# Index products with the roles of their operands exchanged, places computed in the layout of their own item, and the product for the rows to fetch moved between two blocks of matmuls

## What is computed

```python
h = rmsnorm(x, norm1); proj = h @ w_in
x = x + concat(diff_attention(q, k, v), pool_mixer(p)) @ w_out
h = rmsnorm(x, norm2)
logits = h @ w_router + b_router            # 32 experts
topv, topi = top_k(logits, 4); gates = softmax(topv)
for each expert e, for its tokens:          # exact, none dropped
    g = min(h @ w_gate[e] + b_gate[e], 7);  u = clip(h @ w_up[e] + b_up[e], -7, 7)
    y = ((u + 1) * g * sigmoid(1.702 * g)) @ w_down[e] + b_down[e]
    x[token] += gate * y
out = rmsnorm(x, final_norm)
```

## Time and profile before

| | us |
|---|---|
| median of three runs | 2234.3 (2232.83 to 2234.88) |
| span of the profiled execution | 2233.1 |
| TensorE matmuls busy | 2168.6 (97%) |
| VectorE busy | 645.9 |
| ScalarE busy | 613.1 |
| GpSimd busy | 460.4 |

### The profile page before, as it was taken

One profiled execution on the slowest core, in us unless ns is written; L12 is line 12 of the kernel. 1 busy time (PEld: TensorE's weight loads), 2 busy tenths in 40 slices (PEclk: granted clock), 3 DMA queues, 4 the chain that ended last, 5 costly groups with the idle time before them and its releaser, 6 DMA issues.

```text
span 2233.1 us, 30784 instructions
## 1 busy us (share of the span) xinstructions
PE 2168.6 (97%) x10323; PEld 1007.6 (45%) x10324; DVE 645.9 (29%) x1868; ACT 613.1 (27%) x1208; POOL 460.4 (21%) x491
## 2 busy tenths in 40 slices
PE   8999999996999999999999899999999999999996
PEld 4444577543444344344434434434443444444443
DVE  2100599255322223121122212212112221222223
ACT  2000588311222322222223222322123221322223
POOL 1014011223121212212121221221122112122222
PEclk9999999997999999999999999999999999999998
DMA  7100300335568967858869795793889968677775
GB/s 265 44 36 0 116 1 1 103 122 207 201 202 296 361 223 245 303 172 325 304 214 363 229 371 190 246 363 112 328 314 373 359 225 283 252 254 263 258 263 187
DMA packets 150889, 501.08 MB, mean 224 GB/s; under 512 B 10570, under 2 KB 35935, under 8 KB 150303
## 3 DMA queue, kind: packets, MB, share of 16 engines
q1 hardware_dynamic: 115184, 445.20, 51.9%
q0 software_dynamic: 33792, 50.35, 11.0%
q10 hardware_dynamic: 1874, 5.02, 0.6%
HBM read 461.64 MB, written 43.09 MB: 226 GB/s over the span
## 4 chain that ended last, share of the span: by engine, by line
PE 93%; DMA 3%; DVE 2%; issue 1%; ACT 1%; POOL 0%; DVEq 0%; ACTq 0%; SPq 0%; POOLq 0%
PE psum L1566 41%; PE psum L1604 15%; PE psum L1294 10%; PE psum L1355 5%; PE psum L1615 4%; PE psum L1378 3%; PE psum L1344 3%; PE psum L1473 2%; DMA weights<-in_w_down 2%; PE psum L1574 2%; PE psum L1554 1%; PE psum L1627 1%; PE psum L1639 1%; PE psum L1387 1%; DMA weights<-in_w_up 1%
## 5 line engine op out<-in xcount | busy, mean ns | idle before, releaser
L1566 PE MATMUL psum<-weights,work 128*128 128x512 f32 (+2 forms) x3008 | 950.4, 595 | 0.0
L1566 PEld LDWEIGHTS psum<-weights,work 128*128 128x128 f32 (+2 forms) x3008 | 365.8, 159 | 487.6 <-issue 487.2
L642 POOL DMA_INDIRECT residual_rows<-work x184 | 287.6, 1563 | 457.2 <-ACT work L856 410.7
L1604 PE MATMUL psum<-weights,work 128*128 128x512 f32 x768 | 340.0, 595 | 0.0
L598 POOL DMA_INDIRECT work<-normed_rows,work x48 | 49.4, 1030 | 839.9 <-DVE work L1095 778.9
L1294 PE MATMUL psum<-weights 128*128 128x512 f32 x512 | 220.9, 593 | 1.3 <-DVE weights L928 1.3
L1604 PEld LDWEIGHTS psum<-weights,work 128*128 128x128 f32 x768 | 142.1, 190 | 166.2 <-issue 166.2
L1184 DVE TENSOR_SCALAR work<-psum 128x256 f32<-128x256 f32 x188 | 79.7, 424 | 417.8 <-ACT work L825 415.0
L825 ACT ACTIVATE work<-psum 128x256 f32<-128x256 f32 x188 | 71.9, 383 | 379.6 <-PE psum L1566 359.6
L807 ACT ACTIVATE work<-psum 128x512 f32<-128x512 f32 x96 | 57.6, 600 | 426.6 <-PE psum L1473 426.6
L1294 PEld LDWEIGHTS psum<-weights 128*128 128x128 f32 x512 | 96.8, 190 | 122.0 <-issue 120.4
(11 more groups left out here) (214 smaller groups left out, 1708.5 us busy)
## 6 DMA issues: line engine op xcount, KB each, us to landing
weights<-in_w_gate SPq DMA_DIRECT2D x64, 2048.0 KB
weights<-in_w_up SPq DMA_DIRECT2D x64, 2048.0 KB
weights<-in_w_down SPq DMA_DIRECT2D x64, 2048.0 KB, 10.4
weights<-in_w_in SPq DMA_DIRECT2D x8, 768.0 KB, 14.2
residual_rows<-x SPq DMA_DIRECT2D x9, 512.0 KB, 3.8
normed_rows<-work ACTq DMA_DIRECT2D x9, 512.0 KB, 3.9
x<-in_x SPq DMA_DIRECT2D x8, 512.0 KB, 9.6
bias_rows_repeated<-bias_rows SPq DMA_DIRECT2D x4, 1024.0 KB, 10.1
```

The lines of the kernel that those rows point to most:

```text
L642: pl.indirect_dma_start(acc_d[:, :], bass.IndirectOffsetOnAxis(dest[:, b:b + 1], 0), yrow[:, b * BLK:(b + 1) * BLK], None, compute_op=ALU. ...
L1566: mm = pe.matmul(out.rearrange("p (m n) -> p m n", m=2), xT[:, k, lo:lo + cols], wgu[:, :, k, blk * BLK:(blk + 1) * BLK], start=False, sto ...
L1604: mm = pe.matmul(bank(4 + h), actT[:, k, :], wdn[:, k, h * HALF:(h + 1) * HALF], start=False, stop=(k == DT - 1))
```

## The change

- `index` exchanges the operands: the six columns are stationary, `pickT` moves (128 columns). The eight products are laid side by side in the 128*32 mode, four at a time, in two rounds, and leave four partial sums in partitions 32g to 32g+5, by 128 slots. The six columns of the expert come from a fixed buffer `parts_own`, which VectorE fills before each `compare` (one copy more).
- `spread_index` is gone. The 128x128 results are copied to `parts_next`, and one item later to `parts_now`. `own_places` multiplies slices of `parts_now` (stationary) with a few columns of ones and zeros `sel`, only for the layout of the item in hand, between `rows(0)` and `index`: 1 product for 128 tokens, 2 for 64, 2 and 4 for 96, 4 for 32.
- A new product `next_rows` (stationary `parts_next`, 128 columns, one moving column) sums the parts of the token number. It stands between `gate_up_ends(0)` and `gate_up_ends(1)`. `row_numbers` follows it on VectorE, ahead of the four units instead of behind them.
- Before item 0, the row numbers of item 1 have eight products of their own, and places of item 0 are computed inside item 0.
- After the loop, the last item computes its places in VectorE's straight part.

```diff
+            def index(n, own=parts_own, picks=pickT, at=6):
+                pe.wait_ge(s_pick, n + 1)
+                if not isinstance(n, int) or n > 0:
+                    pe.wait_ge(s_own, n)
+                for r in range(2):
+                    for g in range(4):
+                        i = 4 * r + g
+                        mm = pe.matmul(index_out(at)[32 * g:32 * g + 6, :],
+                                       own[:, i, :], picks[:, i, :], start=(r == 0), stop=(r == 1))
+                mm.then_inc(s_ips, 1)
...
+                def place_of(blocks, slots, cols):
+                    n = slots.stop - slots.start
+                    for g in range(P // n):
+                        mm = pe.matmul(places_out[n * g:n * g + n, blocks, :].rearrange("p b c -> p (b c)"),
+                                       parts_now[:, slots], sel[:, cols], start=True, stop=True)
+                    return mm
+
+                def own_places():
+                    if tokens == 128:
+                        mm = place_of(slice(0, 4), slice(0, 128), slice(0, 8))
+                    if tokens == 96:
+                        place_of(slice(0, 2), slice(0, 64), slice(0, 4))
+                        mm = place_of(slice(2, 4), slice(64, 96), slice(6, 10))
+                    if tokens == 64:
+                        mm = place_of(slice(0, 4), slice(0, 64), slice(4, 12))
+                    if tokens == 32:
+                        mm = place_of(slice(0, 4), slice(0, 32), slice(6, 14))
+
+                def next_rows():
+                    pe.wait_ge(s_idxb, j + 3)
+                    pe.wait_ge(s_xT, 2 * j + 3)
+                    pe.matmul(next_out, parts_next, sel[:, 0:1], start=True, stop=True).then_inc(s_gps2, 1)
...
-                pe.wait_ge(s_found, j + 1)
-                spread_index(j + 1)
...
                 rows(0)
-                pe.wait_ge(s_found, j + 2)
-                index(j + 2, bass.ds(e2, 1)).then_inc(s_ips, 1)
+                pe.wait_ge(s_idxb, j + 2)
+                pe.wait_ge(s_found, 2 * j + 2)
+                own_places()
+                index(j + 2)
...
                     gate_up_ends(0)
+                    next_rows()
                     gate_up_ends(1)
```

On VectorE, in the loop:

```diff
-                    places(chain, j + 1, kind)
-
+                    dve.wait_ge(s_ips, j + 3)
+                    places(chain, kind)
+                    chain(dve.tensor_copy(parts_now, parts_next))
+                    dve.tensor_copy(parts_next, index_out(6)).then_inc(s_idxb, 1)
+
+                    dve.wait_ge(s_gps2, j + 1)
+                    row_numbers(chain, next_out)
                     for b in range(UNIT):
-                        if b == 0:
-                            dve.wait_ge(s_ips, j + 3)
-                            index_parts(j + 2)
                         unit(j, b)
-
-                    dve.wait_ge(s_xtp, 2 * j + 3)
-                    row_numbers(chain, idxb[:, 0:3])
+                    dve.wait_ge(s_found, 2 * j + 4)
                     dve.wait_ge(s_added, j + 1)
-                    chain(dve.tensor_copy(dest, nextitem[:, 0:4]))
-                    chain(dve.tensor_copy(dgate, nextitem[:, 4:8]))
-                    shift_places(j + 1)
+                    chain(dve.tensor_copy(dest, later[:, 0:4]))
+                    dve.tensor_copy(dgate, later[:, 4:8]).then_inc(s_dest, 1)
                     item_slots(chain, bass.ds(e3, 1), bass.ds(j + 3, 1))
+                    own_parts(bass.ds(e3, 1)).then_inc(s_own, 1)
                     compare()
```

More of the change, by code:

```diff
@@ L183, in encoder_kernel @@
         idx = small(1).bitcast(U32)
[L184 to L188, removed]
+        new, empty = small(1), small(1)
+        parts_now, parts_next = (small(CHUNK // 2).bitcast(BF16) for _ in range(2))
+        found, lost, later = small(4), small(4), small(8)
         dest = small(4).bitcast(U32)
         dgate = small(4)
-        tables = small(24 + 2 * EXPERTS)
+        tables = small(40 + 2 * EXPERTS)
         place, away, of_row = tables[:, 0:12], tables[:, 12:24], tables[:, 24:24 + EXPERTS]
         of_place = tables[:, 24 + EXPERTS:24 + 2 * EXPERTS]
+        sel_rows = tables[:, 24 + 2 * EXPERTS:]
         items = small(3 * TABLE)[0:1, :].bitcast(I32)
@@ L1089, in compare, with own_parts @@
                                   col.unsqueeze(2).to_broadcast([P, TT, CHUNK]), ALU.is_equal).then_inc(s_pick, 1)
+            def own_parts(e):
+                return dve.tensor_copy(parts_own.rearrange("p i c -> p (i c)"),
+                                       parts_e[:, e, :, :].rearrange("p e i c -> p (e i c)"))
             def row_numbers(chain, src):
-                chain(dve.tensor_reduce(new, src, AX_X, ALU.add))
-                chain(dve.scalar_tensor_tensor(empty, new, 1.0, missing, ALU.is_lt, ALU.mult))
@@ L1094, in row_numbers @@
-                chain(dve.scalar_tensor_tensor(new, new, -1.0, empty, ALU.add, ALU.add))
+                chain(dve.scalar_tensor_tensor(empty, src, 1.0, missing, ALU.is_lt, ALU.mult))
+                chain(dve.scalar_tensor_tensor(new, src, -1.0, empty, ALU.add, ALU.add))
                 dve.tensor_copy(idx, new).then_inc(s_idx, 1)
[L1097 to L1110, removed]
+            def first_row_numbers(src):
+                link(dve.tensor_reduce(new, src, AX_X, ALU.add))
+                row_numbers(link, new)
@@ L1111, in places @@
+            def places(chain, kind):
+                chain(dve.scalar_tensor_tensor(lost, places_out[:, :, 0], 1.0, away[:, bass.ds(kind * 4, 4)],
                                                ALU.is_lt, ALU.mult))
-                chain(dve.scalar_tensor_tensor(found[:, 0, :], found[:, 0, :], float(UNIT),
+                chain(dve.scalar_tensor_tensor(found, places_out[:, :, 0], float(UNIT),
                                                place[:, bass.ds(kind * 4, 4)], ALU.mult, ALU.add))
-                chain(dve.tensor_tensor(later[:, 0:4], found[:, 0, :], lost, ALU.add))
@@ L1222, in _, with last_step @@
             last = dve.value_load(total[0:1, 1:2], min_val=EXPERTS - 1, max_val=MAX_ITEMS - 1)
-            dve.wait_ge(s_rps, n_items + 1)
-            dve.sem_inc(s_found, 1)
+            kind = dve.value_load(items[0:1, bass.ds(n_items + (2 * TABLE - 1), 1)], min_val=0, max_val=KINDS - 1)
+            ended = [0]
+            def last_step(ins):
+                ended[0] += 1
+                ins.then_inc(s_ldve, 1)
+                dve.wait_ge(s_ldve, ended[0])
+            dve.wait_ge(s_ips, n_items + 2)
+            places(last_step, kind)
+            dve.sem_inc(s_idxb, 1)
+            dve.sem_inc(s_idx, 1)
             unit(last, 0)
             unit(last, 1)
+            dve.wait_ge(s_found, 2 * n_items + 2)
             dve.wait_ge(s_added, n_items)
[L1228 to L1231, removed]
+            last_step(dve.tensor_copy(dest, later[:, 0:4]))
+            dve.tensor_copy(dgate, later[:, 4:8]).then_inc(s_dest, 1)
             unit(last, 2)
@@ L1474, in row_transposes @@
                 mm.then_inc(s_xtp, 1)
[L1477 to L1495 removed]
             pe.wait_ge(s_tokid, 3)
             pe.wait_ge(s_lgt, TT)
[L1499 removed]
+            first_rows(0, slice(0, 1), pick0, rows_out)
             pe.wait_ge(s_diag, 4)
```

107 lines of the change are left out of this document (48 added, 59 removed).

## The result

The changed kernel takes 2240.83 us (median of 7 runs, 2239.39 to 2241.61) against 2234.3 before: a ratio of 1.0029, 95% interval 1.002 to 1.0038. The forecast was 2239.4, range 2231 to 2247, with slower as the likeliest case. The profiled execution took 2241.5, of which 2239.3 is its span; before it was 2233.1, so the spans differ by 6.2.

The account below looks back on a forecast made before the run. TensorE, busy 97% of the span, was taken as the bound. Terms -8.3 + 7.4 + 8.5 - 1.2 - 1.3 = +5.1 us on the 2234.3 median gave 2239.4 us; own range 2234 to 2245, 8-in-10 range 2231 to 2247.

Parts of the forecast that it names:

- spread removed: Dropping eight spread products at item boundaries saves 0.18 behind 128 tokens, 0.28 behind 64 or 96, nothing behind 32: -8.3 us.
- places and index: From an item's last transpose to its long product, new place products, index and mode changes add +7.4 us, bounds +3 to +12.
- product for the rows: The added `next_rows` product costs 0.11 in full items, 0.25 between narrow blocks, 0.27 in items of 32: +8.5 us.
- start: Before and in item 0, VectorE's places no longer awaited, item 1's gather an estimated 1.7 earlier: -1.2 us, between -0.5 and -3.
- last item: In the last item the index no longer waits for VectorE's loop exit nor runs 0.76 longer than usual: -1.3 us.
- the 0.33 to 0.40 named as a sign: Expected profile sign: distance from a full item's places to the next long product is 0.33 to 0.40 us.
- The wait ahead of item 0: Expected profile sign: TensorE's wait before item 0 gone, and the one for the gather longer.
- The cheap change (1): Mode changes behind products this short are cheap, at 0.05 us the sum is +0.5: 2235 us; chance 0.14.
- The index in a fourth of the time (2): Four tiles at once make eight index products take 0.05 instead of 0.15, 4.7 us less: 2234.7; chance 0.08.
- Tiles that don't overlap (3): Eight bfloat16 index products run one after another, 0.3 more in each of 47 items, +13: 2252 us; chance 0.04.
- `next_rows` waits (4): `next_rows` holds TensorE's queue for `parts_next`, 0.6 in 8 items, unit 0 as late: +5 to +8, 2246; chance 0.11.
- More from start and end (5): Wait before item 0 gives all 3.0, the end 2, 2.5 beyond the booked; with cheap mode changes 2232 us; chance 0.05.

Follow-up runs that it names:

- again: The changed kernel run once more, unaltered; 2239.86 us, ratio 1.003 to the kernel before.
- no_spread: The kernel before without the eight spread products in its items, a wait and a semaphore increment in their place; 2229.04 us, ratio 0.9981.
- fewer_waits: The changed kernel with one implied TensorE wait at an item's start dropped and another moved behind the rows' transposes; 2238.59 us, ratio 1.002.
- places_last: The changed kernel with the place products behind the eight index products instead of ahead of them; 2238.57 us, ratio 1.0018.
- moved: The changed kernel with the rows product straight ahead of the hidden transposes, in another bank, and row numbers after unit 0; 2233.91 us, ratio 1.0001.
- order: The changed kernel with only VectorE's order altered: row numbers worked out after unit 0 instead of before it; 2242.02 us, ratio 1.0037.
- behind: The changed kernel with the rows product left in place but in another bank with its waits, row numbers after unit 0; 2241.38 us, ratio 1.0032.

## Why the prediction was right, point by point

| Step | booked | measured |
|---|---|---|
| spread removed | -8.3 | -7.2 |
| places and index | +7.4 | +5.6 |
| product for the rows | +8.5 | +8.6 |
| start | -1.2 | -0.4 (-1.0 in **again**) |
| last item | -1.3 | -1.4 |
| sum | +5.1 | +5.2 |

The direction came out, and its reason: TensorE is the bound, and the changes of mode and the cut narrow runs cost more than the spread gave. That the sum agrees to 0.1 is luck. The spread saved 1.1 less than booked and the start 0.8 less, and the places and index cost 1.8 less; these errors cancel. The spans differ by another 1.5 that is chance and was not forecast.

- **The spread.** 0.18 and 0.28 were right behind 128 and 64 tokens (0.18, 0.29). Behind 96 tokens I booked 0.28 as well and got 0.07 to 0.20. The step that failed was that TensorE reaches the bias products as soon as the projections end. In **no_spread** the kernel before does not save it either, and **fewer_waits** brings it back.
- **Places and index.** 24 x 0.13 + 7 x 0.16 + 8 x 0.195 + 8 x -0.03 = 5.6, the split from the rows product worked out with 0.11 and 0.26 for that (0.02 of the 0.13 behind the index is the late first long product, which **places_last** takes away). The term was oversized. Eight turned products and the change into what follows take 0.21 to 0.22, where I booked 0.25; the change is 0.10 and not 0.15 there. From the places of a full item to the long product it is 0.31, just under the 0.33 to 0.40 named as a sign. In items of 32 the places and the index together are 0.02 to 0.03 cheaper than the old index (0.74 against 0.76 from the transposes to the long run, 838.04 and 837.11). Elsewhere the sign holds: 0.20 in one mode became 0.31 with the places.
- **The product for the rows.** 0.11, 0.26 and 0.26 against 0.11, 0.25 and 0.27. In five of the eight items of 32 TensorE waited 0.20 to 0.22 for unit 0 as worked out, before 0.14 to 0.19; in item 0 and one other the unit was in time (0.02), and from index to hidden transposes they lost only 0.02 and 0.07. **moved** takes the loss of the five away.
- **The start.** The step that failed was that the gather for item 1 starts 1.7 earlier. Counted from the first projection, VectorE begins the row numbers 1.0 earlier (554.23 against 554.39, in an execution 0.89 late) and the gather starts 0.8 earlier, as the eight products made for the row numbers delay the transposes for which the gather waits as well. The wait ahead of item 0 did not go, as named for a sign, but shrank to 2.04. And the gather's own length moves the term between executions: from its start to the transposes behind it 8.2 before, 9.3 after, 8.8 in **again**.
- **Rivals.** The cheap change (1): refuted, since a change ahead of the places costs 0.09 and the one that **places_last** saves 0.10 to 0.13. The index in a fourth of the time (2): its mechanism is there by half, its gain is not. In the mode of their surroundings (items of 32) the eight take 0.11 against 0.20 in the old form; with one change behind them they take 0.21 to 0.22. Tiles that don't overlap (3): refuted, as the eight would then take 0.4. `next_rows` waits (4): it did not, with 0.13 to spare. More from start and end (5): refuted.
- By the Trainium skill (TensorEngine Tiling, Key Properties) a change of mode drains the engine. The traces agree in that each change costs time, and give 0.09 to 0.10 us for it here. Its advice (Performance Considerations) to put the narrow operand in the stationary place with column tiling did not pay by the traces of whole-array or 64-column items: places and index cost 0.13 to 0.20 more there than the old index, and 0.02 to 0.03 less only in items of 32, where the work around them is in the same mode.

## What to carry to other kernels

Price a small product by what it does to its neighbours: here the product itself took 0.025 to 0.04 us, a change of tiling mode 0.10, and a narrow run cut in two 0.26. So put small products where the mode changes anyhow, and let the ones in the mode of the next long run come last; in these traces the two moves gave back 8.6 us of the 14.2 by which the items had grown. And where an engine is at 97%, count what its sequencer has to read at a stage's start: behind items of 96 tokens the eight products removed saved half of their 0.28, until two waits that were long over were out of the way as well.

## What the runs showed of the hardware

- A wait whose condition was long met is not free at a point where TensorE's sequencer has no lead over the array: two of them took 0.09 to 0.27 us behind items of 96 tokens, and nothing behind items of 128.
- The final six small products came after a wait of 3.56 or 3.57 us in all twelve traces. They ran at a granted clock of 0.50 (1.2 GHz) in seven, at 0.59 in one and at 0.93 to 1.00 (2.4 GHz) in four, and both levels occur with the same code. They and what follows took 0.6 us more at the lower one.
- In items of 32 tokens, where VectorE worked out the row numbers behind unit 0 and the product for them stood inside the narrow run (**order**, **behind**), ScalarE began its copy of the hidden transposes 0.92 to 1.05 us after their start in most items (0.75 in one). In two items of each of these traces it was 0.42, and in the other traces 0.34 to 0.50, but for one item of **moved** (0.77). The cause is open.
